# Layer one's x loaded by columns instead of transposed, and two later transposes moved from TensorE to VectorE

## The reference

```
hn = x * rsqrt(mean(x^2) + 1e-6) * pre_norm_g[i]        # before each layer
layer 0:  q, k, v, z = split(hn @ w_in)                  # 2048 x 8192
          y = (attention(rope(q), rope(k), v) * silu(z)) @ w_out
layer 1:  a, g, z = split(hn @ w_in)                     # 2048 x 6144, bias on a and g
          u = conv31(a * sigmoid(g)) + b_dw
          y = (silu(layer_norm(u)) * silu(z)) @ w_out + b_out
x = x + rms_norm(y) * post_norm_g[i]                     # after each layer
```

## Time and the profile before

| | |
|---|---|
| median of 3 runs | 840.01 us (839.89 to 840.35) |
| profiled execution, and its span | 840.96 us, 839.2 us |
| TensorE matmuls | 829.8 us busy, 3,807 of them |
| VectorE, ScalarE, GpSimd busy | 713.0, 426.3, 343.1 us |
| mean granted TensorE clock | 0.997 |
| moved by DMA | 161.62 MB, 193 GB/s |

### The profile page before, as it was taken

One profiled execution on the slowest core, in us unless ns is written; L12 is line 12 of the kernel. 1 busy time (PEld: TensorE's weight loads), 2 busy tenths in 40 slices (PEclk: granted clock), 3 DMA queues, 4 the chain that ended last, 5 costly groups with the idle time before them and its releaser, 6 DMA issues.

```text
span 839.2 us, 10950 instructions
## 1 busy us (share of the span) xinstructions
PE 829.8 (99%) x3807; PEld 687.6 (82%) x3807; DVE 713.0 (85%) x1234; ACT 426.3 (51%) x589; POOL 343.1 (41%) x173
## 2 busy tenths in 40 slices
PE   9999999999999999999999999999999999999996
PEld 6888888888888888888888888888888888888885
DVE  5688799988999799979847649999999999898655
ACT  6744535455444734454446574444545454575542
POOL 0343005500441004500000198888888878894001
PEclk9999999999999999999999999999999999999998
DMA  9956656656567555756455485556555646566522
GB/s 316 318 157 202 193 150 177 195 181 196 154 176 224 171 178 153 219 175 243 171 195 197 150 285 192 182 195 200 182 172 198 200 151 201 196 215 246 196 100 100
DMA packets 97945, 161.62 MB, mean 193 GB/s; under 512 B 3348, under 2 KB 38772, under 8 KB 97396
## 3 DMA queue, kind: packets, MB, share of 16 engines
q1 hardware_dynamic: 97572, 160.87, 59.3%
q10 hardware_dynamic: 336, 0.28, 0.1%
HBM read 159.04 MB, written 2.10 MB: 192 GB/s over the span
## 4 chain that ended last, share of the span: by engine, by line
PE 98%; DMA 0%; DVE 0%; ACT 0%; issue 0%; DVEq 0%; POOL 0%; SPq 0%
PE acc L459 29%; PE acc L460 29%; PE acc L461 29%; PE X L469 1%; PE acc L444 1%; PE acc L446 1%; PE acc L445 1%; PE X L459 1%; PE X L460 1%; PE X L461 1%; PE acc L525 1%; PE acc L540 1%; DMA xrow<-in_x 0%; PE acc L779 0%; PE acc L778 0%; PE acc L777 0%
## 5 line engine op out<-in xcount | busy, mean ns | idle before, releaser
L806 ACT ACTIVATE w_hi<-raw 128x1024 fp32r<-128x1024 f32 x282 | 298.6, 1060 | 339.3 <-PE acc L461 326.5
L459 PE MATMUL acc<-w_hi,xT_hi 128*128 128x512 f32 x864 | 339.1, 392 | 0.0
L461 PE MATMUL acc<-w_hi,xT_lo 128*128 128x512 f32 x864 | 336.9, 390 | 0.0
L460 PE MATMUL acc<-w_lo,xT_hi 128*128 128x512 f32 x864 | 336.7, 390 | 0.0
L1112 DVE TENSOR_TENSOR w_lo<-raw,w_hi 128x1024 fp32r<-128x1024 f32 x180 | 242.2, 1362 | 69.6 <-ACT w_hi L806 67.2
L1609 POOL TENSOR_TENSOR w_lo<-raw,w_hi 128x1024 fp32r<-128x1024 f32 x102 | 248.4, 2443 | 45.1 <-ACT w_hi L806 45.0
L461 PEld LDWEIGHTS acc<-w_hi,xT_lo 128*128 128x128 f32 x864 | 162.3, 188 | 33.9
L459 PEld LDWEIGHTS acc<-w_hi,xT_hi 128*128 128x128 f32 x864 | 162.4, 188 | 33.2 <-DVE xT_lo L1131 0.3
L460 PEld LDWEIGHTS acc<-w_lo,xT_hi 128*128 128x128 f32 x864 | 162.4, 188 | 32.7
L1402 DVE SCALAR_TENSOR_TENSOR X<-u_pad,taps,X 128x256 f32<-128x256 f32 x464 | 183.7, 478 | 3.5 <-ACT X L1019 3.5
L1572 POOL TENSOR_TENSOR small<-small 128x1 f32<-128x1 f32 (+1 forms) x7 | 4.3, 618 | 221.5 <-DVE small L1329 122.9
(11 more groups left out here) (165 smaller groups left out, 800.4 us busy)
## 6 DMA issues: line engine op xcount, KB each, us to landing
raw<-in_w_in SPq DMA_DIRECT2D x78, 1024.0 KB, 5.3
raw<-in_w_in SPq DMA_DIRECT2D x66, 512.0 KB, 4.5
raw<-in_w_out SPq DMA_DIRECT2D x32, 1024.0 KB, 5.1
gpost<-in_post_g SPq DMA_DIRECT2D x2, 1024.0 KB, 5.7
brow<-in_b_in SPq DMA_DIRECT2D x1, 2048.0 KB, 10.4
out<-xrow SPq DMA_DIRECT2D x6, 256.0 KB, 2.8
xrow<-in_x SPq DMA_DIRECT2D x4, 256.0 KB, 5.9
raw<-in_w_in SPq DMA_DIRECT2D x4, 256.0 KB, 4.5
```

Of the source, the lines that this page charges most:

```text
L459: nc.tensor.matmul(a, hi[:, k, rows], w_hi[:, slot, i], start=(k == 0), stop=False)
L460: nc.tensor.matmul(a, hi[:, k, rows], w_lo[:, slot, i], start=False, stop=False)
L461: last = nc.tensor.matmul(a, lo[:, k, rows], w_hi[:, slot, i], start=False, stop=(k == KT - 1 or n == pause))
L806: nc.scalar.activation(w_hi[:, slot], raw[:, u % LOADS, 2 * half:2 * half + 2], ACT.Copy).then_inc(hi_ready[slot], 1)
```

## The change

x is also given to the kernel turned (`x_cols`, features on the partitions, made on the host from the input), and so are the vectors and the taps. Layer one's `xT_hi` and `xT_lo` are made straight from the loaded `x_col`, and TensorE's transposes of x, vectors and taps are gone. The rows of x, still needed for the squares and the residual, are loaded later, in four transfers, two each ahead of loads 5 and 6. Three slices instead of two go tile by tile and seven of eight, instead of four, in passes. The squares go behind slices 9 and 11 on ScalarE, the eviction of q behind slice 12, its turn on VectorE from slice 17. In layer two, the last pair of x1 and the first gated pair are turned by VectorE in 16 pieces of 32x128 each, and the first taps of pair 0 stand behind slice 15's weights instead of slice 13's.

```diff
-SPLIT_AFTER = ((), (), (2,), (3,), (4, 5), (6,), (7, 8), (9,))
-FINE = 2
-SQUARES_AFTER = (1, 2, 3, 5)
-STAGED = 4
+X_CHUNKS = ((0, 1), (1, 2), (2, 4), (4, 8), (8, 12), (12, KT))
+ROW_SQUARES_AT = {9: (0, 1), 11: (2, 3)}
+FIRST_MEAN_AT = 11
+FIRST_EVICT_Q, FIRST_TURN_Q = 12, 17
+SPLIT_AFTER = ((), (), (), (3,), (4, 5), (6,), (7, 8), (9,))
+FINE = 3
+STAGED = 7
+X1_TURNS = ((0,), (1,), (2, 3))
...
+            col_load(0)
             w_load(0, 0, 0, tile_in[0])
             w_load(0, 1, 1, tile_in[1])
+            col_load(2)
             w_load(0, 2, 2, tile_in[2])
             w_load(0, 3, 3, raw_ready[0])
+            col_load(3)
+            w_load(1, 0, 0, tile_in[3])
+            w_load(1, 1, 1, half_in[0])
             w_load(1, 2, 3, raw_ready[1])
+            col_load(4)
+            w_load(2, 0, 1, half_in[1])
+            w_load(2, 2, 3, raw_ready[2])
+            col_load(5)
+            w_load(3, 0, 1, half_in[2])
+            w_load(3, 2, 3, raw_ready[3])
             load(S_QKVZ, 0, 32, 4, w_in0[0], D)
+            row_load(0)
+            row_load(1)
+            load(S_QKVZ, 0, 32, 5, w_in0[0], D)
+            row_load(2)
+            row_load(3)
             sp.dma_start(cos_t[:], rope_cos).then_inc(rope_in, 16)
             sp.dma_start(sin_t[:], rope_sin).then_inc(rope_in, 16)
             sp.dma_start(mask[:], causal).then_inc(rope_in, 16)
+            load(S_QKVZ, 0, 32, 6, w_in0[0], D)
+            for j in range(7, 16):
                 load(S_QKVZ, 0, 32, j, w_in0[0], (j // 4) * D)
+                if j == 8:
+                    sp.dma_start(ident[:], identity).then_inc(ident_in, 16)
+                    sp.dma_start(taps[:], tap_cols).then_inc(taps_in, 16)
...
-                tile_products(0)
-                input_T(0, 1)
-                tile_products(1)
-                tile_products(2)
-                input_T(0, 2)
-                tile_products(3)
-                input_T(0, 3)
+                for t in range(2 * FINE):
+                    tile_products(t)
...
-            keep_clock(4)
-            pe.wait_ge(ident_in, 16)
-            pe.wait_ge(pre_in, 16)
-            nc.tensor.transpose(X[3][:, 0:NPRE], pre_rows[:], ident[0:NPRE, 0:NPRE]).then_inc(vec_T, 1)
-            keep_clock(3)
-            input_T(0, 0)
-            keep_clock(2)
+            keep_clock(8)
             first_block()
...
-                if h + 2 < SLICES:
-                    input_T(1, h + 2)
+                if h + 2 < SLICES - 1:
+                    input_T(h + 2)
...
-                    if s == (9 if first else 11):
-                        conv_input_pair(2 * i, 0, first)
+                    if s == 11 and not first:
+                        conv_input_pair(2 * i, 0)
...
+            def column_high(h):
+
+                act.wait_ge(col_in[col_chunk(2 * h)], 16)
+                for t in (2 * h, 2 * h + 1):
+                    last = nc.scalar.activation(xT_hi[:, t], x_col[:, t], ACT.Copy,
+                                                scale=vec[:, V_PRE0 + t:V_PRE0 + t + 1])
+                last.then_inc(xhi_ready, 1)
...
+            act.dma_start(vec[:], vectors).then_inc(vec_in, 16)
+            a, b = X_CHUNKS[1]
+            act.dma_start(x_col[:, a:b], x_cols[:, a:b]).then_inc(col_in[1], 16)
+            act.wait_ge(const_set, 2)
+            nc.scalar.activation(small[:, 112:114], m_half, ACT.Copy)
+            act.wait_ge(vec_in, 16)
...
+            def first_squares(n):
+
+                act.wait_ge(row_in[n], 16)
+                for m in range(MT):
+                    squares(junk0[:], xrow[:, m, n * NCOL:(n + 1) * NCOL], m, n, MT * n + m)
...
-            input_high(1, 7, V_PRE1)
+            act.wait_ge(x1_turned, 4)
+            for c in range(2):
+                t = 2 * (SLICES - 1) + c
+                last = nc.scalar.activation(xT_hi[:, t], x1T[:, c], ACT.Copy, scale=vec[:, V_PRE1 + t:V_PRE1 + t + 1])
+            last.then_inc(xhi_ready, 1)
...
-                act.wait_ge(agT_done, e + 1)
                 if e == 0:
                     act.wait_ge(pad_set, 1)
+                    act.wait_ge(taps_in, 16)
+                    act.wait_ge(pair0_turned, 4)
+                    act.sem_inc(upad_ready, 1)
...
-                if at == (5 if e == 0 else 7):
+                if at == 7:
                     first_taps(e)
...
+            def turn_pair(dst, row, a, done):
+
+                for b in range(4):
+                    last = nc.vector.transpose(
+                        dst[b * BLK:(b + 1) * BLK].rearrange("p h (m c) -> p m h c", m=MT)
+                        [:, :, :, a * BLK:(a + 1) * BLK],
+                        row[a * BLK:(a + 1) * BLK].rearrange("p m (h c) -> p m h c", h=2)
+                        [:, :, :, b * BLK:(b + 1) * BLK])
+                last.then_inc(done, 1)
...
-            for h in range(RING, SLICES):
-                input_low(1, h, V_PRE1)
+            for h in range(RING, SLICES - 1):
+                for a in X1_TURNS[h - RING]:
+                    turn_pair(x1T, xrow[:, :, (SLICES - 1) * SEQ:D], a, x1_turned)
+                input_low(h)
...
             rows_biased(0)
             glu(0)
+            dve.wait_ge(glu_ready, 1)
+            for a in range(4):
+                turn_pair(u_pad[:, 0:2, PAD:UW], ag_row[:, 0, :, 0:SEQ], a, pair0_turned)
```

More of the change, by code:

```diff
@@ L489, in acc_free, with input_T @@
                     pe.wait_ge(y_ready, MT * (o - 31))
[L491 to L510, removed]
+            def input_T(h):
+                for m in range(MT):
+                    pe.wait_ge(x1_ready[m], h + 1)
+                pe.wait_ge(xlo_ready, units(h - 4, 1))
+                pair_T(xrow, X[h % 4], 2 * h).then_inc(xT_done, 1)
             def staged_products(h):
@@ L607, in group @@
                         values(g - 1)
[L608 to L615, removed]
                     if s == SCORES_AT:
-                        if first:
-                            pe.wait_ge(vec_ready, 2)
-                        else:
+                        if not first:
                             pe.wait_ge(u_ready, g)
@@ L794, in high @@
                 slot = s % RING
[L795 to L796 removed]
+                if isinstance(it, int) and first + it == 0 and s in (2, 4, 6):
+                    act.wait_ge(half_in[s // 2 - 1], 16)
                 else:
@@ L920, in group @@
                         group_end(s, g - 1)
-                    if s == 12 and first:
-                        act.wait_ge(vec_T, 2)
-                        nc.scalar.activation(vec[:, NPRE:NPRE + NVEC], X[1][:, 0:NVEC], ACT.Copy)
-                        nc.scalar.activation(taps[:], X[0][:, 0:TAPS * KT], ACT.Copy).then_inc(vec_ready, 1)
-                    if s == 11:
+                    if first:
+                        for n in ROW_SQUARES_AT.get(s, ()):
+                            first_squares(n)
+                    if s == (FIRST_EVICT_Q if first else EVICT_Q):
                         if first:
@@ L1132, in input_low, with column_low @@
                         out=xT_lo[:, t], in0=X[n % 4][:, c * SEQ:(c + 1) * SEQ],
-                        scalar=vec[:, vcol + t:vcol + t + 1], in1=xT_hi[:, t].bitcast(f32),
+                        scalar=vec[:, V_PRE1 + t:V_PRE1 + t + 1], in1=xT_hi[:, t].bitcast(f32),
                         op0=ALU.mult, op1=ALU.subtract)
+                last.then_inc(xlo_ready, 1)
+            def column_low(h):
+                dve.wait_ge(xhi_ready, h + 1)
+                for t in (2 * h, 2 * h + 1):
+                    last = nc.vector.scalar_tensor_tensor(
+                        out=xT_lo[:, t], in0=x_col[:, t], scalar=vec[:, V_PRE0 + t:V_PRE0 + t + 1],
+                        in1=xT_hi[:, t].bitcast(f32), op0=ALU.mult, op1=ALU.subtract)
                 last.then_inc(xlo_ready, 1)
@@ L1259, in group @@
                     low(S_QKVZ, g, 32, s)
+                    if s == FIRST_MEAN_AT and first:
+                        mean_of_parts(8, 1)
+                        dve.wait_ge(rope_in, 48)
                     if not first:
                         group_end(s, g - 1)
-                    if s in range(TURN_Q, TURN_Q + 4):
-                        if s == TURN_Q:
+                    turn_q = FIRST_TURN_Q if first else TURN_Q
+                    if s in range(turn_q, turn_q + 4):
+                        if s == turn_q:
                             dve.wait_ge(rope_step, 6 * g + 3)
@@ L1283, in out0_rows @@
                     dve.wait_ge(gpost0_in, 16)
+                    for n_in in range(NG):
+                        dve.wait_ge(row_in[n_in], 16)
                 for m in ms:
@@ L1361, in _ @@
             row_low(3, 1)
-            for h in range(RING, SLICES):
-                input_low(1, h, V_PRE1)
             for m in range(MT):
                 dve.wait_ge(x1_ready[m], SLICES)
+            for h in range(RING, SLICES - 1):
+                for a in X1_TURNS[h - RING]:
```

(9 more changed lines are left out.)

183 lines of the change are left out of this document (81 added, 102 removed).

## The result

The changed kernel takes 841.25 us (median of 16 runs, 840.74 to 842.66) against 840.03 for the kernel before beside it (16 runs, 839.28 to 841.15): ratio 1.0016, 95% interval 1.0008 to 1.0023. That is 1.2 us slower where 1.4 us faster was forecast, and just inside the upper end of the range (841.3). The profiled execution has 840.75 us around a span of 838.8.

A forecast was written before the change was run, and what follows sets the result against it. TensorE, with 98% of the chain, was taken as the bound. Layer one's −2.9 us and +1.45 for the two VectorE turns summed to −1.4, so 838.6 us by the median; range for 8 in 10: 836.0 to 841.3.

The forecast's parts named there:

- Part 1: Layer one by columns: TensorE's transposes go, load 4 holds slice 7, slice 10 starts at 36.6; gain 2.9 us.
- the bounds given for it: Layer one: load 4 lands between 24.0 and 26.5, giving a gain of 4.1 to 1.6 us.
- the prediction's own limits: Layer one: the prediction is wrong if slice 10 starts elsewhere than 35.4 to 37.9.
- The late pieces of part 1: Squares, q's eviction and turn, identity and taps moved later: nothing, or a few tenths that slices of lead hide.
- Part 2: x1's last pair: TensorE loses a 0.49 us group; VectorE's 16 turns cost nothing, up to 0.9 us at 0.44 each.
- Part 3: First gated pair: VectorE's taps start 4.3 us later against the slices, so TensorE stalls 2.4 us at pair 1.
- The net of +1.45: At pair 1: TensorE runs 1.45 us later than layer one's change left it, the two groups' 0.98 included.
- The clock: Rival, chance 0.09: TensorE's clock falls at pair 1 if the stall is some 3.5 us, losing 3 us; 842.7.

The follow-up runs named there:

- before_again: The kernel before, unchanged, run once more for a second trace: 839.80 us, ratio 0.9998.
- x1_pe: Changed kernel with x1's last pair turned by TensorE again, the rest of the change kept: 840.24 us, ratio 0.9995.
- x1_psum: Changed kernel with x1's last pair still turned by VectorE, but into PSUM bank 3 instead of SBUF: 839.39 us, ratio 0.9989.
- pair0_pe: Changed kernel with gated pair 0 turned by TensorE again and its first taps behind slice 13's weights: 840.16 us, ratio 0.9993.
- part1_alone: Changed kernel with x1's last pair and gated pair 0 both turned by TensorE again, layer one as changed: 836.95 us, ratio 0.9961.

## Why the prediction was wrong

**Part 1, forecast −2.9: the size came out, in part by luck.** 839.92 to 836.95 and 840.01 to 837.01 are −3.0 both times by the medians. The wait was the right one, slice 7's x tiles behind load 4, but two terms were off and cancelled. Load 4 landed at 23.55, not 25.2, and outside the bounds given for it (24.0 to 26.5): ScalarE starts on its weights there, released by it:

```profile
23.55 1.06 ACT L791 ACTIVATE w_hi<-raw 128x1024 fp32r<-128x1024 f32 x1 [1.25 <-DMA raw<-in_w_in]
```

Slice 7 starts at 26.71, not 28.4, and slice 10 at 35.01, not 36.6, outside the prediction's own limits. Slice 7 is 4.1 us ahead of where it stands in the profiled execution of before. But this execution was not typical: its first products run at half pace, in the profile of before_again they don't (first product at 6.16, x1's pair 7 turned at 488.11 instead of 489.41, 839.68 us in all). 1.3 us of the 4.1 belong to that slow start, which most runs of before don't have in full (840.96 us against a median of 840.01). Slice 10, where the forecast counted its gain, starts at 39.39 in the first profile and at 38.04 in that of before_again:

```profile
38.04 0.48 PE L459 MATMUL acc<-w_hi,xT_hi 128*128 128x512 f32 x1
```

With the 0.1 of slow matmuls, the gain at slice 10 is 4.5 us against the first profile and 3.1 against the second, and 3.0 is what the medians give. In the changed kernel a slow start costs less, for TensorE then waits for load 4 anyway: slice 7 starts at 26.98 in x1_pe with a slow start, at 26.65 in x1_psum with a quick one. The late pieces of part 1 (squares, eviction and turn of q, identity) cost nothing that shows, as forecast: VectorE's 2.3 us of waiting for q is hidden.

**Part 2, "Cost nothing": this step failed.** It counted the turns, which were right (0.32 us against 0.305), and asked only if the low part of pair 6 comes in time behind them. It does, and takes 0.88 as in the earlier trace rows; its input is still in PSUM. The low part of the turned pair itself, pair 7, has no term in the sum. With x1T in SBUF it takes 4.28 instead of 0.88, slice 7 waits 2.13, and the part costs 2.1 − 0.5 = 1.6 us: pair0_pe's group at 838.6 against 837.0. The prediction cites the very rule for the gate, whose two inputs lie in SBUF in both kernels, and does not ask it of the one instruction whose operand the change moves.

**Part 3, a stall of 2.4 us: right.** It is 2.33 us at pair 1, and in no later pair. The first taps' 1.06 us stand behind slice 15's weights, VectorE's taps start at 506.13 and the gate ends at the turn. The part alone costs 2.33 − 0.49 = 1.84: x1_pe's group at 838.8. Without the wait the turn would stand at 525.75; the gate starts 1.4 us behind that (forecast 1.5) and is 0.78 long, bound by the end of POOL's instruction (forecast 0.8 for that reason). The net of +1.45 for parts 2 and 3 together was too small only by part 2's hole. That the second hole does not swallow the first is plain from x1_pe and x1_psum, which have the same 2.33 without it: the taps' slot is tied to the slices, so both move together.

**The clock, given 0.09 and 3 us: it does fall behind stalls, but condition and size were wrong.** It was to decide from a stall of 3.5 us; it comes behind 2.1 and 2.3 us, in 5 of 16 runs here and in 8 of 11 of x1_pe, and costs 1.6. Here it moves the median by 0.3 (840.98 for the eleven, 841.25 for all). Behind which of the two holes it fell in the five is not on record.

**Sum.** −3.0 + 1.6 + 1.85 + 0.3 = +0.75, measured +1.2. Some 0.2 of the 0.45 left over is time outside the span: its median is 2.09 us in the 16 runs of the changed kernel and 1.85 to 1.90 in part1_alone, x1_pe and pair0_pe, from which the parts are sized. Why it is longer, and the rest, are not explained. How often the clock falls behind a hole differs between kernels with equal holes, and I have not tried what sets it.

## What to carry to other kernels

When a change moves an operand from PSUM to SBUF, price again the instructions that read it, not only those that write it: beside a busy GpSimd two VectorE instructions went from 0.88 to 4.28 us. A hole in TensorE costs its length and, in part of the runs, a stretch at half clock behind it, so look at single times and clocks before medians, and try idle matmuls in a hole that can't be closed. When several parts are in one change, run each alone: here one was worth 3 us and two together cost more than it, and a gain taken against one profiled execution should be held against a second one of the same kernel.

## What was not expected of the hardware

The clock fell behind holes as short as 2.1 us (pair0_pe, 490.23), down to 1.2 GHz for a little over 3 us. With nine idle matmuls of 0.23 us in the hole it fell in none of eleven runs, on another chip than that of x1_psum, where it fell in six of eleven. A VectorE transpose of 32x128 costs 0.32 us whether it goes to SBUF (2.54 for eight) or, nearly, to PSUM (2.70 for eight).
